# GpSimd makes every other low part of the first expert table, in quarters; VectorE's dots on gathered rows read x from PSUM

## What is computed

```python
q = (xc @ wq).reshape(PEER_CHUNK, PEER_HEADS, 2, PEER_HALF)
s = jnp.einsum('chpd,hpkd->chpk', q, subkeys).astype(jnp.float32)
...
ug = jnp.take(u_table, eidx, axis=0)
vg = jnp.take(v_table, eidx, axis=0)
hid = jnp.einsum('cd,chkd->chk', xc, ug).astype(jnp.float32)
a = jax.nn.gelu(hid, approximate=False) * g
return jnp.einsum('chk,chkd->cd', a.astype(vg.dtype), vg)
```

## Time and profile before

| | us |
|---|---|
| median of 3 runs | 2487.85 (2487.5 to 2489.3) |
| the profiled execution, its time | 2487.53 |
| its span in the profile | 2485.7 |
| TensorE busy | 2457.6 |
| VectorE busy | 1797.5 |
| ScalarE busy | 1167.2 |
| GpSimd busy | 533.0 |

### The profile page before, as it was taken

How to read it: one execution, slowest core, us unless ns; L and a number is a source line. 1 busy time by engine, 2 the same in 40 slices (tenths; PEclk the granted TensorE clock), 3 DMA queues, 4 the chain that set the end, 5 groups by cost and what they waited for, 6 DMA issues and landing times.

```text
span 2485.7 us, 35461 instructions
## 1 busy us (share of the span) xinstructions
PE 2457.6 (99%) x13593; PEld 2232.8 (90%) x13593; DVE 1797.5 (72%) x3334; ACT 1167.2 (47%) x1970; POOL 533.0 (21%) x342
## 2 busy tenths in 40 slices
PE   8999999999999999999999999999999999999998
PEld 7788888999999999999999999888888888888887
DVE  7876678998998886798898887877786335533323
ACT  6555466467767786333333334544422224422222
POOL 3222065132322342365554400000000000000000
PEclk9999999999999999999999999999999999999999
DMA  4211345588988998999999982222474323223331
GB/s 170 69 58 46 119 153 168 194 315 317 323 301 295 342 394 335 390 390 390 392 392 391 388 288 85 86 97 85 139 268 156 102 94 102 85 93 102 101 99 38
DMA packets 191239, 519.15 MB, mean 209 GB/s; under 512 B 15896, under 2 KB 67096, under 8 KB 187872
## 3 DMA queue, kind: packets, MB, share of 16 engines
q1 hardware_dynamic: 154208, 382.66, 43.8%
q0 software_dynamic: 36864, 134.23, 14.7%
HBM read 464.34 MB, written 52.49 MB: 208 GB/s over the span
## 4 chain that ended last, share of the span: by engine, by line
PE 88%; DVE 8%; ACT 3%; issue 1%; DMA 0%; DVEq 0%; SPq 0%; ACTq 0%
PE P L1295 27%; PE P L1297 27%; PE P L1296 27%; PE P L1642 2%; DVE wl L1754 1%; PE P L1302 1%; ACT wh L2405 1%; DVE T L1754 1%; DVE D L1754 1%; DVE RW L1754 0%; DVE RU L1754 0%; DVE T L1757 0%; PE P L1575 0%; PE P L1574 0%; PE P L1573 0%
## 5 line engine op out<-in xcount | busy, mean ns | idle before, releaser
L1295 PE MATMUL P<-XH,wh 128*128 128x512 f32 (+2 forms) x2272 | 845.1, 372 | 4.9 <-DVE QK L1757 2.5
L1297 PE MATMUL P<-XH,wl 128*128 128x512 f32 (+2 forms) x2272 | 823.1, 362 | 0.0
L1296 PE MATMUL P<-XL,wh 128*128 128x512 f32 (+2 forms) x2272 | 822.4, 362 | 0.0
L2405 ACT ACTIVATE wh<-raw 128x1024 fp32r<-128x1024 f32 x458 | 482.1, 1056 | 348.3 <-PE P L1297 340.2
L1754 DVE TENSOR_TENSOR wl<-raw,wh 128x1024 fp32r<-128x1024 f32 x420 | 509.2, 1220 | 75.0 <-ACT wh L2405 74.6
L1295 PEld LDWEIGHTS P<-XH,wh 128*128 128x128 f32 x2272 | 428.1, 188 | 50.0 <-issue 4.6
L1297 PEld LDWEIGHTS P<-XH,wl 128*128 128x128 f32 x2272 | 427.1, 188 | 47.6
L1296 PEld LDWEIGHTS P<-XL,wh 128*128 128x128 f32 x2272 | 428.0, 188 | 42.6 <-issue 1.9
L1295 PE MATMUL P<-AH,wh 128*128 128x384 f32 x1024 | 342.8, 335 | 1.3 <-DVE wl L1754 1.3
L1297 PE MATMUL P<-AH,wl 128*128 128x384 f32 x1024 | 342.1, 334 | 0.0
L1296 PE MATMUL P<-AL,wh 128*128 128x384 f32 x1024 | 342.1, 334 | 0.0
(11 more groups left out here) (329 smaller groups left out, 3269.2 us busy)
## 6 DMA issues: line engine op xcount, KB each, us to landing
raw<-wts SPq DMA_DIRECT2D x211, 512.0 KB, 3.6
raw<-ut SPq DMA_DIRECT2D x128, 512.0 KB, 6.5
raw<-vt SPq DMA_DIRECT2D x128, 512.0 KB, 12.0
hdram<-HID SPq DMA_DIRECT2D x64, 384.0 KB, 4.6
gdram<-GS SPq DMA_DIRECT2D x24, 1024.0 KB, 6.2
GI<-gdram SPq DMA_DIRECT2D x16, 1536.0 KB, 16.3
HI<-hdram SPq DMA_DIRECT2D x32, 768.0 KB, 16.7
AWC<-adat SPq DMA_DIRECT2D x64, 256.0 KB, 5.2
```

The lines of the kernel that those rows point to most:

```text
L1295: e.matmul(bank, wh[:, w], H, start=start, stop=False)
L1296: e.matmul(bank, wh[:, w], L, start=False, stop=False)
L1297: return e.matmul(bank, wl[:, w], H, start=False, stop=stop)
L2405: return e.activation(dst, src, ACT.Copy)
```

## The change

Three things are changed together.

- Low parts: from unit 20 of the first table up to unit 120, every second unit's low part (51 of them) is GpSimd's. For units of the first table it is made by four subtractions of 256 columns, with one semaphore count at the last.
- x for the dots: the eight PSUM banks become one tensor `PS`, and banks 4 and 5 hold a copy of `XT` (`XTP`) that VectorE makes half by half in `rows`. The 116 dots of this stage read it there; the 12 late dots go on reading `XT`.
- Banks: the first table's units use banks 0 to 2 instead of 0 to 3, `gate_turn` uses bank 3 instead of 4, and the second table's waits (`v_bank`) are set to match: bank 1 now waits for the gelu of the first table's last unit, banks 4 and 5 for the last of the 116 dots.

```diff
--- before.py
+++ after.py
@@ -50,7 +50,8 @@
 
 
 def low_on_pool(i):
-    return 5 <= i < U_WQ and i - U_OUT not in (4, 5) or U_WQ + 4 <= i < U_U
+    return 5 <= i < U_WQ and i - U_OUT not in (4, 5) or U_WQ + 4 <= i < U_U \
+        or U_U + 20 <= i < U_V - 6 and i % 2 == 1
 
 
 
@@ -839,7 +840,8 @@
         XH = at("XH", 60, [128, 8, T], F32R)
         XL = at("XL", 76, [128, 8, T], F32R)
         TB = [at(f"T{i}", 92 + 2 * i, [128, T], F32) for i in range(7)]
-        P = [ctx.enter_context(nc.psum_tensor(f"P{i}", [128, T], F32)) for i in range(8)]
+        PS = ctx.enter_context(nc.psum_tensor("PS", [128, 8 * T], F32))
+        P = [PS[:, T * i:T * i + T] for i in range(8)]
         G1, G2, GF, GM, GN, GE = (sm[:, 8 * i:8 * i + 8] for i in range(6))
         ADB, CW, BF = sm[:, 48:96], sm[:, 96:120], sm[0:8, 120:121]
         SH_M, GT_M, SH_F, GT_F = mod[:, 0:8], mod[:, 16:24], mod[:, 24:32], mod[:, 40:48]
@@ -899,6 +901,7 @@
         IOP = at("IOP", F + 84.25, [128, 16, 2], F16)
         HID = [at(f"HID{i}", F + 84.75 + 3 * i, [128, 2, ND], F32) for i in range(2)]
         XT = at("XT", F + 90.75, [128, 1024], F32)
+        XTP = PS[:, 4 * T:6 * T]
         CAN = at("CAN", F + 75, [128, 8, 80], F32)
         OE = [at(f"OE{i}", F + (60, 62, 98.75)[i], [128, 2, 2, 128, 2], F16) for i in range(3)]
         OM = [at(f"OM{i}", 96 + 2 * i, [128, 2, 2, 128, 2], F16) for i in range(2)]
@@ -1342,20 +1345,20 @@
 
             def u_bank(u):
                 i = u - U_U
-                if i < 4:
+                if i < 3:
                     p.wait_ge(s_qpl, 13 + i)
                 else:
-                    p.wait_ge(s_gelu, i - 3)
-                return i % 4
+                    p.wait_ge(s_gelu, i - 2)
+                return i % 3
 
             def v_bank(d):
-                if d < 4:
-                    p.wait_ge(s_gelu, 125 + d)
-                elif d == 4:
+                if d < 3:
+                    p.wait_ge(s_gelu, (127, 128, 126)[d])
+                elif d == 3:
                     p.wait_ge(s_it, 3)
                     p.wait_ge(s_gtv, 3)
-                elif d == 5:
-                    p.wait_ge(s_keyc, 16)
+                elif d < 6:
+                    p.wait_ge(s_rows, 1 + 128 - LATE)
                 else:
                     p.wait_ge(s_gs, 89 + d)
 
@@ -1615,13 +1618,13 @@
 
             def gate_turn(tb):
                 if tb == 0:
-                    p.wait_ge(s_keyc, 16)
+                    p.wait_ge(s_qpl, 16)
                 else:
                     p.wait_ge(s_gtv, tb)
                     p.wait_ge(s_it, tb)
                 p.wait_ge(s_gate, tb + 1)
                 for n, src in enumerate((IS[:, 0, :], IS[:, 1, :], GR[:, tb, :])):
-                    t = e.transpose(P[4][:, n * 128:n * 128 + 128], src, ident[:, :])
+                    t = e.transpose(P[3][:, n * 128:n * 128 + 128], src, ident[:, :])
                 t.then_inc(s_gt, 1)
 
             def grid(n):
@@ -2048,6 +2051,10 @@
                 w = slice(512 * half, 512 * half + 512)
                 v.wait_ge(s_sc, 17 + half)
                 tt(XT[:, w], P[7][:, :], XT[:, w], ALU.add).then_inc(s_qpl, 1)
+                v.wait_ge(s_qpl, 17 + half)
+                v.wait_ge(s_keyc, 16)
+                step(e.tensor_copy(XTP[:, w], XT[:, w]).then_inc(s_v, 1))
+                last["xtp"] = step.n
 
             def sparse_index():
                 own()
@@ -2057,9 +2064,9 @@
 
             def dot(n):
                 b = GB[n % 4]
-                v.wait_ge(s_qpl, 18)
+                v.wait_ge(s_v, last["xtp"])
                 v.wait_ge(d_row[n % 4], 16 * row_count(n))
-                e.tensor_tensor_reduce(out=b[:, :], in0=b[:, :], in1=XT[:, :], scale=1.0, scalar=0.0, op0=ALU.mult,
+                e.tensor_tensor_reduce(out=b[:, :], in0=b[:, :], in1=XTP, scale=1.0, scalar=0.0, op0=ALU.mult,
                                        op1=ALU.add, accum_out=HS[:, n:n + 1]).then_inc(s_rows, 1)
 
             def dot_late(r):
@@ -2084,7 +2091,7 @@
 
             def gate_turn(tb):
                 q = slice(tb * 32, tb * 32 + 32)
-                src = P[4][:, 256:384].rearrange("p (n t) -> p n t", t=4)
+                src = P[3][:, 256:384].rearrange("p (n t) -> p n t", t=4)
                 rest = GTL[tb % 2][:, :].rearrange("p (n t) -> p n t", t=4)
                 v.wait_ge(s_it, tb + 1)
                 if tb == 2:
@@ -2594,7 +2601,7 @@
             def gate_turn(tb):
                 c.wait_ge(s_gt, tb + 1)
                 copy(IT[:, 32 * tb:32 * tb + 32, :, :].rearrange("p n a t -> p a n t"),
-                     P[4][:, 0:256].rearrange("p (a n t) -> p a n t", a=2, t=4)).then_inc(s_it, 1)
+                     P[3][:, 0:256].rearrange("p (a n t) -> p a n t", a=2, t=4)).then_inc(s_it, 1)
 
             def weigh(n):
 
@@ -2626,7 +2633,7 @@
                 c.wait_ge(s_used, U_U + i + 1)
                 if n >= 2:
                     c.wait_ge(d_hid[n % 2], 16 * (n // 2))
-                e.activation(HID[n % 2][:, i % 2, :], P[i % 4][:, 0:ND], ACT.Gelu).then_inc(s_gelu, 1)
+                e.activation(HID[n % 2][:, i % 2, :], P[i % 3][:, 0:ND], ACT.Gelu).then_inc(s_gelu, 1)
 
 
             def activate_(i):
@@ -2785,8 +2792,12 @@
                     wait_room(g, i)
                     if LOW_COUNT[i] > 1:
                         g.wait_ge(s_low_p, LOW_COUNT[i] - 1)
-                    e.tensor_tensor(WL[i % NW][:, :], RAW[i % NRAW][:, :], WH[i % NW][:, :].bitcast(F32),
-                                    ALU.subtract).then_inc(s_low_p, 1)
+                    n = 4 if U_U <= i < U_V else 1
+                    for j in range(n):
+                        w = slice(1024 // n * j, 1024 // n * (j + 1))
+                        t = e.tensor_tensor(WL[i % NW][:, w], RAW[i % NRAW][:, w], WH[i % NW][:, w].bitcast(F32),
+                                            ALU.subtract)
+                    t.then_inc(s_low_p, 1)
                     last["low"] = LOW_COUNT[i]
 
             def fill():
```

## The result

The changed kernel takes 2495.69 us (median of 7 runs, 2494.89 to 2498.24) against 2487.85 before; the ratio is 1.0032, with a 95% interval of 1.0022 to 1.0041. Its profiled execution took 2494.89 us, its span is 2493.1, 7.4 longer than before. The forecast of 2495.7 was right by the total, but by luck: one part that was put at 4 us is nothing, and one that was put at 0.3 is 4.4.

What follows compares the result with a forecast made beforehand. VectorE was taken to set the pace before 495 us, TensorE (99% busy) afterwards. Terms 0.8 + 2.5 + 0.3 + 4 + 0.3 = 7.9 us on 2487.53 gave 2495.4, median 2495.7; range 2489 to 2506.

Steps and rivals of the forecast that it cites:

- (a): Two copies of x into PSUM in VectorE's stream, at 420.6 and 426.3 us, delay TensorE: +0.8 us (0.6 to 1.5).
- (b): GpSimd's low part of unit 20, about 486.5 us: its quarters get between VectorE's two-SBUF-input operations, +2.5 us (0 to 3).
- (c): 500 to 835 us: VectorE and GpSimd both have room; +0.3 us for a one-hot tile that comes late.
- (d): 835 to 970 us: gathers queued behind GpSimd's low parts leave late and delay dots and one-hot tiles, +4 us (0 to 20).
- (e): Start of the second table: its first unit waits for bank 1, which holds the last unit's result, +0.3 us (0.1 to 1.5).
- rival 4: VectorE's waits for quarters eat the 62 us, busy 500 to 970 stays near 422, (d) upper half; counted in rival 2.
- rival 1: The last stretch absorbs GpSimd's load: (d) 0 to 1, time 2491.8 to 2492.7; chance 0.34 together with (b) small.
- Rival 2: GpSimd becomes the bound after 835 us: (d) 10 to 20, time 2502 to 2512; chance 0.17.
- Rival 3: Faster: TensorE's 6.4 us of waits for low parts before 495 us go away, 2481.5; faster by over 0.2%: 0.04.
- The sign for (c): TensorE waiting for its banks (a gelu) would show that the three banks were wrongly costed at nothing.

Runs made afterwards that it cites:

- Experiment 7: Changed kernel with each GpSimd quarter waiting for the one before, and GpSimd's low parts from unit 22 instead of 20: 2489.15 us, ratio 1.0005 to the kernel before.
- experiment 1: Changed kernel without GpSimd's low parts of the first table (VectorE makes all), keeping x in PSUM, its copies and three banks: 2489.46 us, ratio 1.0003.
- experiment 9: Kernel before the change, with GpSimd making the low parts of first-table units 7, 8, 14, 15, 16 in chained quarters: 2483.69 us, ratio 0.9982.
- Experiment 3: Changed kernel with chained quarters: each GpSimd quarter waits for the count of the one before: 2492.57 us, ratio 1.0017 to the kernel before.
- experiment 2: Changed kernel with GpSimd's low parts from unit 22 on instead of 20, one fewer: 2494.57 us, ratio 1.0026 to the kernel before.
- experiment 5: Changed kernel with GpSimd's low parts from unit 88 to 120 only, 17 of them: 2489.27 us, ratio 1.0004 to the kernel before.

## Why the prediction was right in its sum and wrong in its parts

| part | forecast | measured |
|---|---|---|
| (a) copies | 0.8 | 0.8 by unit 13 (0.70 us each) |
| (b) low part of unit 20 | 2.5 | 1.9 at unit 18 |
| (c) 500 to 835 us | 0.3 | 4.4 at units 45 to 56 |
| (d) 835 to 970 us | 4 | 0 |
| (e) bank 1 | 0.3 | 0.4 |
| sum | 7.9 | 7.5; less 0.1 by which the execution came early to unit 0: 7.4 |

**The bound.** Read rightly: TensorE had idle time before 495 us only, and the 51 low parts that the change moves lie behind it. Experiment 7 with the relief is 0.4 us longer in span than experiment 1 without it, so the relief is worth nothing, as said; experiment 9 shows the same reading from the other side: relief in the right 60 us gives 4.2.

**(a), (e).** As forecast. "VectorE has no idle time between there and 493 us" was not quite so: it has two gaps of 0.38 us before, at 440 and 475 us, in which it waits for ScalarE, but they took up nothing of the delay. The two copies in the changed kernel's groups of 415 to 432 us, and the wait for bank 1 in its waits of 1000 to 1010 us:

```profile
L2056 DVE COPY PS<-XT 128x512 f32<-128x512 f32 x2 | 1.4, 696 | 0.1
```

```profile
PEld PS L1298 <- ACT HID L2636: 0.4, 1, 0.4
```

**(b).** The mechanism holds, f16 operations wait as well: `D` at 487.56 took 1.64 instead of 1.23 us, the low part behind it 1.75.

```profile
487.14 5.47 POOL L2798 TENSOR_TENSOR wl<-raw,wh 128x256 fp32r<-128x256 f32 x4 [22.83 <-ACT wh L2412]
...
487.56 1.64 DVE L1757 TENSOR_TENSOR D<-D,IF 128x2048 f16<-128x2048 f16 x1
489.13 1.75 DVE L1757 TENSOR_TENSOR wl<-raw,wh 128x1024 fp32r<-128x1024 f32 x1
```

The Trainium skill (SBUF — State Buffer, Who interferes with whom) says that a VectorE instruction with two SBUF inputs contends with a GpSimd one that reads SBUF, and sets no condition on the type; here the trace agrees. In VectorE's stream the delay reached 2.6 us at 494 us, copies included. TensorE got it in two waits within unit 18: for the low part, as forecast (1.25 us instead of 0.29), and, which the prediction did not have, for the indices `IS` that it transposes there (1.34 instead of 0.40). Before, then now, from 425 to 495 us:

```profile
PE P L1624 <- DVE IS L1754: 0.4, 1, 0.4
...
PE PS L1627 <- DVE IS L1757: 1.3, 1, 1.3
```

**(c), the step that failed.** "Room on both. I put +0.3 for a moment in which a one-hot tile comes late." Two things in it were wrong. The 44 us that VectorE would get back were not there: it is busy 305.5 of 335 us instead of 304.4, so rival 4's condition came true, though not what it said of (d). And a wait was taken to be at most one quarter; but the rows of the kernel before have GpSimd's work as single instructions, and quarters that follow at once can act on an operation like one of 2.8 us. Experiment 3 shows that it hangs on the close succession: with a gap, six `OM` that began 0.1 to 0.3 us before the first quarter waited for one (1.1 to 1.35 us), two more for none, and none for all four. The place is where VectorE has its routing work beside the one-hot tiles. In the kernel before, three times there (at 617, 627 and 658 us) the products of line 1642 come only 1.5 to 2.5 us after the end of the last `OM` that they read, and 2.6 to 7 us after it elsewhere. The exceptions are at 509 and 518 us (1.5 and 0.4); at the first of these experiment 2 lost its 0.7.

**(d), the other one.** "A gather behind a low part leaves up to 3.7 us late, and the turn has 1.8 in hand." The gathers' own durations were taken over from before, and they fell. For the earlier trace rows, the changed kernel's, 835 to 975 us:

```profile
L2836 POOL DMA_INDIRECT GB<-un,SI x46: 932/956/1756, 835.1 to 967.3; - x46
...
DMA to landing us min/median/max: 5.8/8.1/11.0
```

A turn needs 0.3 + 8.1 + 1.2 = 9.6 us, so 2.7 of 12.3 are in hand. VectorE's waits for gathers grow, as forecast, from 3.2 to 5.9 us; but the low parts that it no longer makes cover that, and the next link, the one-hot product, is not late. That was rival 1. What makes the difference is x in PSUM, which the prediction costed at nothing in the dots (right: 1.209 against 1.216 us) and credited with nothing in (d): with x in SBUF and chained quarters the same stretch loses 8.2 us, and without GpSimd's low parts (experiment 1) VectorE waits 0.2 us there for gathers where it waited 3.2 before. For quarters without a gap x in SBUF was not run.
The Trainium skill (VectorE: DVE Perf Modes, The TRN2 errata) has 120 cycles against 58 as the fixed part for a PSUM source, by the prediction's estimate 0.065 us a dot; the dots, one input in each memory, don't show it.

**The range and the rivals.** (c) and (d) missed by about the same amount in opposite directions: the total came out by luck and proves neither. Rival 1 held in its place, and alone it would have given 2492. Rival 2 didn't occur: GpSimd is busy 96 of 135 us, since 13 low parts there took 3.5 us each (2.8 to 4.0) and a gather's issue 1.14 us in the mean instead of 1.34. One of its conditions was also added up wrongly: with 0.5 us of waiting a quarter, 14 low parts come to 68 us, not 55 to 60. Rival 3 was rightly all but excluded.

**The checks that were named.** TensorE's waits for `wl` did grow before 500 us, by 3.1 (from 6.4 to 9.5, matmuls and weight loads together), and a quarter took 0.74 us. TensorE without idle time from 835 to 970 us was named as the sign against (d). The sign for (c) was looked for at the banks, where nothing was found, not at the one-hot products.

## What to carry to other kernels

Before work is moved off an engine, look where the bound engine is idle at all: 51 low parts moved behind that place gave nothing, and with what they needed cost 7.4 us; five moved into it gave 4.2. Work that was cut up so that a neighbour can get in between needs a gap between the pieces: here a wait for the piece before was enough. When a sum comes out right, compare its terms one by one with the trace.

## What the runs showed of the hardware that was not expected

- Cutting a GpSimd instruction into pieces that follow at once does not always let VectorE in between. Nine `OM` of the changed kernel, both inputs in SBUF, began 0.1 to 0.3 us before the first of four quarters and were held to the end of the fourth: 3.2 to 3.4 us instead of 0.42. With each quarter waiting for the one before (0.08 us between them) no `OM` took over 1.36 us in three kernels. What decides when there is no gap was not settled, and it is not the position alone: `OE` that began 0.02 to 0.17 us before a first quarter were never held so in the changed kernel, and four in experiments 2 and 5 that began 0.04 to 0.25 us after one were. The Trainium skill (SBUF — State Buffer, Who interferes with whom) says that issue order decides who blocks; with the `OM` the operation whose record begins first was the one to wait, perhaps because its record begins before it reads, which no row tells.
- The issue of an indirect DMA on GpSimd took 0.94 to 0.96 us from 835 us on where no VectorE operation with two SBUF inputs ran beside it, and up to 1.8 before the change. In the mean it took 1.34 to 1.38 us in the four kernels whose dots read x from SBUF and 1.14 to 1.26 in the others. The cause was argued from this, not tested by itself.
- The same idle time of TensorE (2.3 of the 4 us from 490 us on) was followed by a clock of 1.00 in one execution and by means of 0.84, 0.70 and 0.57 over the next 4 us in three others. The 0.70 cost about 1.2 us.
